# Gating products of the second output pass moved from DVE to GpSimd, with the row look-ups issued between them

## The reference

```python
def _peer(hn, w_query, sub_keys, expert_u, expert_v):
    ...                                   # top 16 of 16384 experts for each of 8 heads and each token
    gate = jax.nn.softmax(cv, axis=-1)
    ...
    def block(args):
        xt, it, gt = args
        u = expert_u[it]
        pre = jnp.einsum('tkd,td->tk', u, xt, preferred_element_type=jnp.float32)
        act = (jax.nn.gelu(pre, approximate=False) * gt).astype(xt.dtype)
        return jnp.einsum('tk,tkd->td', act, expert_v[it])
```

## Time and profile before

| | |
|---|---|
| three executions | 4584.95, 4588.24, 4594.18 us |
| the profiled execution, own time | 4578.11 us |
| its span (first to last instruction) | 4576.5 us |
| PE busy | 4120.9 us, 90% |
| DVE busy | 2536.3 us, 55% |
| POOL busy | 1985.2 us, 43% |
| ACT busy | 1315.9 us, 29% |
| mean granted clock of TensorE | 0.952 of full speed |

### The profile page before, as it was taken

The page is one execution under the profiler, slowest core; times in us unless marked ns, Lnnn a source line. Parts: engine busy times, 40 slices in busy tenths (PEclk is TensorE's granted clock), DMA queues, the critical chain, the costliest instruction groups (busy, mean ns, idle before and its releaser), DMA issues.

```text
span 4576.5 us, 55934 instructions
## 1 busy us (share of the span) xinstructions
PE 4120.9 (90%) x19920; PEld 3445.6 (75%) x19920; DVE 2536.3 (55%) x4788; ACT 1315.9 (29%) x1806; POOL 1985.2 (43%) x1384
## 2 busy tenths in 40 slices
PE   7958688988879889899899998999999999988988
PEld 5824487868657668799789987998888888776776
DVE  5453467676223441467667776776544444566666
ACT  2013232322121221333233332333322222323233
POOL 1022123332000000178788777788888887010110
PEclk9979898989989999999999999999999999999999
DMA  2249200000120012266666665665777778677775
GB/s 97 96 184 380 74 17 8 16 8 9 74 97 23 32 46 82 81 171 184 156 173 176 175 174 145 176 193 146 183 193 190 192 189 233 228 273 258 275 262 204
DMA packets 373200, 672.10 MB, mean 147 GB/s; under 512 B 153440, under 2 KB 227168, under 8 KB 355552
## 3 DMA queue, kind: packets, MB, share of 16 engines
q1 hardware_dynamic: 207200, 469.10, 30.5%
q0 software_dynamic: 165888, 201.86, 18.3%
HBM read 522.50 MB, written 148.31 MB: 147 GB/s over the span
## 4 chain that ended last, share of the span: by engine, by line
PE 37%; DMA 7%; POOL 4%; DVE 4%; issue 3%; ACT 1%; DVEq 1%; SPq 1%; ACTq 0%; POOLq 0%
PE peer_ps L1975 19%; PE peer_ps L2024 18%; DMA peer_gat<-gates_d 6%; POOL gates_d L1932 4%; DMA peer_rows<-in_expert_uv,peer_idx 2%; DVE peer_acc L2266 1%; ACT peer_vh L2092 1%; DVE peer_al L2284 1%; DVEq L2265 0%; SPq L1883 0%; DVE rows L2251 0%; ACT peer_uh L2092 0%; DVE peer_ul L2174 0%; PE peer_ps L2016 0%; DVE peer_rows L2251 0%
## 5 line engine op out<-in xcount | busy, mean ns | idle before, releaser
L1932 POOL DMA_INDIRECT gates_d<-peer_gates,peer_idx x896 | 1500.8, 1675 | 324.7 <-issue 267.2
L1975 PE MATMUL peer_ps<-high,peer_uh 128*128 128x448 f32 x2048 | 594.6, 372 | 65.5 <-DVE peer_ul L2174 47.7
L1975 PE MATMUL peer_ps<-low,peer_uh 128*128 128x448 f32 x2048 | 590.9, 370 | 0.0
L1975 PE MATMUL peer_ps<-high,peer_ul 128*128 128x448 f32 x2048 | 589.6, 369 | 0.0
L1975 PEld LDWEIGHTS peer_ps<-high,peer_uh 128*128 128x128 f32 x2048 | 389.5, 191 | 103.8 <-DVE peer_ul L2174 50.8
L2024 PE MATMUL peer_ps<-peer_vh,peer_ah 128*128 128x512 f32 x1198 | 378.9, 398 | 45.1 <-DVE peer_al L2284 45.1
L1975 PEld LDWEIGHTS peer_ps<-low,peer_uh 128*128 128x128 f32 x2048 | 391.5, 191 | 33.7
L1975 PEld LDWEIGHTS peer_ps<-high,peer_ul 128*128 128x128 f32 x2048 | 389.7, 190 | 33.3
L2024 PE MATMUL peer_ps<-peer_vh,peer_al 128*128 128x512 f32 x1198 | 376.4, 396 | 0.0
L2024 PE MATMUL peer_ps<-peer_vl,peer_ah 128*128 128x512 f32 x1198 | 375.9, 395 | 0.0
L2280 DVE TENSOR_TENSOR peer_vl<-peer_val,peer_vh 128x1024 fp32r<-128x1024 f32 x171 | 209.7, 1227 | 245.1 <-ACT peer_vh L2092 244.3
(11 more groups left out here) (432 smaller groups left out, 7318.8 us busy)
## 6 DMA issues: line engine op xcount, KB each, us to landing
peer_val<-in_expert_uv SPq DMA_DIRECT2D x256, 512.0 KB, 3.7
gates_d<-mla_zeros POOLq DMA_DIRECT2D x128, 512.0 KB
peer_raw<-in_expert_u SPq DMA_DIRECT2D x128, 512.0 KB
hidden_d<-peer_hid SPq DMA_DIRECT2D x128, 448.0 KB, 2.8
peer_act_in<-hidden_d SPq DMA_DIRECT2D x128, 256.0 KB, 4.2
peer_gat<-gates_d SPq DMA_DIRECT2D x128, 256.0 KB, 4.7
peer_act_in<-hidden_d SPq DMA_DIRECT2D x128, 192.0 KB, 3.9
peer_gat<-gates_d SPq DMA_DIRECT2D x128, 192.0 KB, 4.5
```

The costliest lines, as they stand in the source:

```text
L1932: pool.indirect_dma_start(gates_flat, bass.IndirectOffsetOnAxis(ap=idx[:, n, k:k + 1], axis=0), gates[:, n, k:k + 1], None, compute_op=ALU ...
L1975: last = nc.tensor.matmul(ps[i][:, a, 0:HD], w[:, cols], x[:, kc, a * HD:(a + 1) * HD], start=(kc == 0 and w is uh[i % 2] and x is high), ...
```

## The change

Before, DVE does all 256 gating products. Now it does the first 128, and POOL does the 128 of the second pass (128x384 each), with a semaphore of their own, `product_late`, for which ACT (before `ah`) and DVE (before `al`) wait. POOL's program interleaves them with the look-ups: the first eight late look-ups as before, then one product a step; after the product of the step that follows a `row_sums`, the two look-ups that those sums allow.

```diff
--- before.py
+++ after.py
@@ -1806,8 +1806,8 @@
             "sums_full", "half_out", "other_out", "squared", "rooted", "inverted", "scaled_out", "out_stored"))
         sc_used, cv_ready, gate_exp, idx_ready, iota_ready = (st.sem(x) for x in (
             "sc_used", "cv_ready", "gate_exp", "idx_ready", "iota_ready"))
-        gain_ready, rows_full, rows_taken, pre_done, gel_done, row_used = (st.sem(x) for x in (
-            "gain_ready", "rows_full", "rows_taken", "pre_done", "gel_done", "row_used"))
+        product_late, gain_ready, rows_full, rows_taken, pre_done, gel_done, row_used = (st.sem(x) for x in (
+            "product_late", "gain_ready", "rows_full", "rows_taken", "pre_done", "gel_done", "row_used"))
         row_squared, row_rooted, row_inverted, row_done = (st.sem(x) for x in (
             "row_squared", "row_rooted", "row_inverted", "row_done"))
         block = st.block()
@@ -1958,8 +1958,18 @@
                     for p in range(turn, upto):
                         look_up(p)
                     turn = upto
-            for p in range(EARLY_SLOTS, SLOTS):
+            ahead_rows = EARLY_SLOTS + RING_OUT
+            for p in range(EARLY_SLOTS, ahead_rows):
                 look_up(p)
+            for q in range(NK, 2 * NK):
+                n = len(PASSES[1]) * P
+                pool.wait_ge(in_ready[q % 2], 48 * (q // 2 + 1))
+                nc.gpsimd.tensor_tensor(act_in[q % 2][:, 0:n], act_in[q % 2][:, 0:n], gat[q % 2][:, 0:n],
+                                        ALU.mult).then_inc(product_late, 1)
+                g = sums_at.get(NK + q - 1, -1)
+                if g * GROUP >= EARLY_SLOTS and g * GROUP + RING_OUT < SLOTS:
+                    for p in range(g * GROUP + RING_OUT, g * GROUP + RING_OUT + GROUP):
+                        look_up(p)
             for tile in range(4):
                 pool.wait_ge(added[tile], scatters(PH - 1, tile + 4 if tile + 4 < DENSE else tile))
 
@@ -2085,12 +2095,13 @@
                     nc.scalar.activation(gel[:, part], pre[:, part], ACT.Gelu).then_inc(gel_done, 1)
 
             def highs_out(q):
+                product_of = (product, q + 1) if q < NK else (product_late, q + 1 - NK)
                 act.wait_ge(in_ready[q % 2], 48 * (q // 2 + 1))
                 n = len(PASSES[q // NK]) * P
                 if q >= RING:
                     taken(act, q - RING)
                 nc.scalar.activation(vh[q % RING][:, :], val[q % 2][:, :], ACT.Copy).then_inc(v_high, 1)
-                act.wait_ge(product, q + 1)
+                act.wait_ge(*product_of)
                 nc.scalar.activation(ah[q % RING][:, 0:n], act_in[q % 2][:, 0:n], ACT.Copy).then_inc(a_high, 1)
 
             def halves(p):
@@ -2280,7 +2291,10 @@
                 nc.vector.tensor_tensor(vl[q % RING][:, :], val[q % 2][:, :], vh[q % RING][:, :].bitcast(F32),
                                         ALU.subtract)
                 dve.wait_ge(a_high, q + 1)
-                dve.wait_ge(product, q + 1)
+                if q < NK:
+                    dve.wait_ge(product, q + 1)
+                else:
+                    dve.wait_ge(product_late, q + 1 - NK)
                 nc.vector.tensor_tensor(al[q % RING][:, 0:n], act_in[q % 2][:, 0:n], ah[q % RING][:, 0:n].bitcast(F32),
                                         ALU.subtract).then_inc(split_done, 1)
 
@@ -2335,7 +2349,8 @@
             for q in range(2, 2 * NK):
                 if q == NK + RING - 1:
                     others(0)
-                multiply(q)
+                if q < NK:
+                    multiply(q)
                 lows_out(q)
                 for n, piece in pieces_of(NK + q - 2):
                     choose(n, piece)
```

## The result

The median of the changed kernel is 4605.01 us (4589.65 to 4616.8, 14 runs), that of the kernel before in the same comparison 4589.64 us (4574.74 to 4599.06, 14 runs). The ratio is 1.0034, with a 95% interval of 1.0022 to 1.0046: the change makes the kernel slower by 0.34%, 15 us, where 4604 us was forecast.

What follows compares the result with a forecast made beforehand. The prediction took the second pass to be bound by a loop of load, conversion, `split_done` and next load. 10 x 1.1 + 10 x 0.5 = 16 us, less 0.5 us, took 4588.24 us to 4604 us; range 4580 to 4632 us.

Steps and rivals of the forecast that it cites:

- The bound: Second pass, about 3940 to 4564 us: a loop of load, conversion, `split_done` and next load sets the time, not PE.
- POOL's product: A 128x384 product on POOL takes 0.95 us, bounds 0.557 to 1.264 us, and costs nothing in a plain step.
- The new wait: DVE's row work at +1 and +3: DVE gives up 0.97 us to POOL, saves 0.46: net 0.5 us later.
- The look-ups: Queued behind POOL's product: first look-up 1.8 us later in turns of the first kind, 0.5 us in the second.
- The forecast's floor: Landing at the next +0 can't move by less than its issue, 0.5 us, unless the later look-ups let it pass.
- The turns: Turns of five steps, 25 us before, ten of each kind: 1.1 us longer in the first, 0.5 in the second.
- The delay at +1 ends in slack: Lateness at +1 only delays the load for +3, where DVE is still adding rows, so it costs nothing.
- The sum: 10 x 1.1 + 10 x 0.5 = 16 us, less 0.5 us once: 4604 us, 0.35% slower.
- 0.5 us to be saved once: Where DVE normalizes the first pass's output and POOL does the product meanwhile, 0.5 us saved once.
- Rival 1: POOL's reads don't hold DVE up and look-ups hardly matter: 10 us faster, 4578 us; chance 0.10.
- Rival 2: Later look-ups stand less in the way of the next +0 landing: 0 to 8 us, 4588 to 4596; chance 0.21.
- Rival 3: POOL's request beats `al` at +0, which waits a product: 20 x 1.0 us more, 4631 us; chance 0.14.

Runs made afterwards that it cites:

- e7: Kernel before, with each of a step's three loads issued as soon as its own buffer is free: 4563.99 us, ratio 0.9933.
- e3: Kernel before, with POOL doing the second-pass products at +0, +2 and +4 only, DVE +1 and +3, look-ups at their old place: 4593.80 us, ratio 1.0005.
- e1: Changed kernel's POOL program with two memsets replacing each product, DVE keeping all products; against the kernel before: 4596.23 us, ratio 1.0014.
- e2: DVE keeps all products, POOL multiplies spare tiles nobody waits for, look-ups behind as in the change; against the kernel before: 4625.96 us, ratio 1.0075.
- e5: Kernel before, with POOL doing second-pass products except at +3, which DVE keeps; look-ups at their old place: 4586.91 us, ratio 0.9989.
- e6: Changed kernel, but DVE keeps the product at +1; look-ups behind the product at +3; against the kernel before: 4601.65 us, ratio 1.0017.
- e4: Changed kernel with each look-up pair issued behind the product of the next +0 instead of +3: 4618.35 us, ratio 1.0061.
- e9: Early loads, DVE doing all products, second look-up of each pair held until `vh` of the next +0 is made: 4572.19 us, ratio 0.9945.
- e10: Kernel before with only the second look-up of each pair held until `vh` of the next +0 is made: 4602.07 us, ratio 1.0019.

## Why the prediction was right

**The bound.** Right. The stage goes by landings: e7, which only issues loads earlier, gains 24 us in 19 turns and 26 us by the medians (31 by the ratio of the runs).

**POOL's product, 0.95 us (0.557 to 1.264).** 1.00 to 1.02 us in a plain step, 1015 ns in e3: 0.06 us more. The Trainium skill's ratio (GPSIMD Engine Reference, §3.1) had given an estimate of 1.09 us, 7% above what the trace shows. That plain steps pay nothing for it is confirmed by e3 and by L2-al2, 2.24 us before and after.

**The new wait, net 0.5 us at +1 and at +3.** That the two engines take turns is right; the size is too large, and at +3 it works in part in another way. At +1 `al` is 0.36 us late (4.36 to 4.72), since the row operation stands 0.81 us (2.03 for 1.22) and 0.46 us are saved. The forecast's stand of 0.97 us isn't worked out in it; its own rows would have given 0.80 us: 1.06 us of a product that takes 1.264 alone is 84%, not one whole product, and 84% of 0.95 is 0.80. The "2.1 to 2.3 us" that I expected of single operations is 2.03, and more only at +4.

At +3 `al` is 0.32 us late in turns of the first kind and 0.21 in those of the second. In the second kind it is as forecast, POOL between the two sums, which stand 0.59 us in five of nine turns and 0.74 in the one shown; less 0.46 us that leaves 0.1 to 0.3. In the first kind it isn't: in six of ten turns no operation of DVE stands at +3 at all. `vl` waits for `vh` there and keeps its 1.23 us, and `al` is late because the landing of +3 is (in the mean of the first kind 3.10 us behind `al` of +2 instead of 2.81), whose load was issued behind the late `al` of +1. In the other four POOL's product, which begins inside the second sum, ends at 4.24 to 4.58 us behind `al` of +2, where DVE's own ended at 3.83. That POOL's reads are the reason for the stands is shown by e1 and e2 together: as much work of POOL's without reads leaves the row operations at 1220 ns.

**The look-ups, 1.8 and 0.5 us later.** Measured 1.70 and 0.47 us, means of the two kinds. In the first kind 0.66 us (al3-next L0 from 10.47 to 11.13) arrive at the next landing beyond what `al` at +3 is late. In the second it is 0.35 us (10.01 to 10.36), but the second execution of the kernel before has 10.35 there, so that nothing of it is clear of the scatter. The forecast's floor, that the landing can't move by less than its issue, isn't borne out: in e5 the issue is 0.4 us later and the landing is not.

**The turns, 1.1 and 0.5 us longer.** 0.96 us (25.10 to 26.06) and 0.52 us (25.13 to 25.65; 0.18 beside the 25.47 of the second execution). The middle taken for the first kind was nearly right, but its makeup was not quite as I put it: I had given the 0.5 us of the collision as the floor and the look-ups as what adds to it; it is 0.32 us up to `al` at +3 and 0.66 us behind it, and the run with late look-ups alone (e1) has 0.5 us of it, the run with a late `al` alone (e5) nothing. By the stretch the experiments build the sum in steps: 2 to 4 us for late look-ups alone (e1), 8 to 10 us with the collision at +3 (e6), 14 us for all. By the runs the steps are 6, 8 and 15 us, each within 5 to 6 us.

**"The delay at +1 ends in slack".** Not as it was put: in turns of the first kind it reaches `al` at +3, since `vl` waited for its landing there in seven of ten turns already. The turn of the earlier trace rows is one of the three in which it didn't. It is the next landing that doesn't follow (e5). For the second kind it isn't settled: nothing by e5's runs, up to 5 us by its 19 turns.

**The sum.** 0.75 us a turn in 19 turns, where 16 us in 20 turns (0.8) were forecast; 15.4 us by the medians. (The forecast's 15.5 us are 0.34%, not 0.35.) Of the 0.5 us to be saved once nothing shows: from step 128 to step 140, with one turn of look-ups in it, both kernels take 70.7 us. That the total lies within 1 us of the forecast is in part luck: the stands were put too high, the delay at +1 at nothing, and what the look-ups add was the middle between two bounds, of which the lower one doesn't hold.

**The rivals.** Rival 1 (POOL's reads don't hold DVE up) fell with 1604 ns for 1220. The contention rule of the Trainium skill (SBUF — State Buffer, "Who interferes with whom"), by which it had to fall, agrees with 2.03 us for 1.22 here. Rival 2 (the landing stands less in the look-ups' way) holds in part: of 1.70 us of lateness 0.66 arrive, of 0.47 between 0 and 0.35. Rival 3 (`al` at +0 stands) doesn't occur, by little: POOL starts 0.02 to 0.32 us behind `al` in the 19 turns (4210.40 against 4210.25 in the one shown), and `al` keeps its 0.55 us. In e2 POOL is some 0.1 us earlier, and `al` takes 1.35 us in 15 of 19 turns, in a kernel of 4626 us, though it isn't the only collision there.

## What to carry to other kernels

Before an operation goes from DVE to POOL, mark in the trace where its request will fall: beside a DVE operation that reads two tiles of SBUF it cost most of its own length here (0.81 of 1.0 us), beside idle DVE nothing, so some steps can be moved and others not (e3), though a move off the path gains nothing either. Look for slack in every turn and not in one: the turn read for the forecast had it at +3, and seven of the ten of its kind had none. Count what is queued behind it on POOL, look-ups above all, and don't take it for granted that a big transfer is cheaper elsewhere: in this stage, set by landings, moving or splitting it only made another load late (e4, e9, e10). Where loads set the pace, let each go out when its own buffer is free: that gave 26 us here, where the change cost 15.

## What was unexpected

A look-up's instruction on POOL, 1.41 us before, takes 1.76 to 1.94 us right behind a product, and the second of the pair 0.94 to 1.31 us. Two memsets of 128x512 on POOL (0.527 us each) leave DVE's operations of two inputs at 1220 and 1285 ns. At +4 `vl` takes 1.7 to 2.5 us instead of 1.23 in 12 of the 19 turns, and the next landing at +1 doesn't show it (2.29 us behind that of +0, 2.26 before). And with early loads the change costs nothing by the runs (0.9939 against 0.9933), with more collisions than without.
